# A hybrid decoder step on one core: adaLN products with the weights streaming, feature chunks further apart, and some steps of the mix phase moved

## The reference

```
shift, scale, gate = split(silu(c) @ w_ada + b_ada, 3)          # c: 9 conditions (1 prompt, 8 samples), w_ada 1024 x 3072
h = rmsnorm(x, norm_gain) * (1 + scale) + shift
qa, ka, va, za, qb, fb, ib, zb, ga, gb = split(h @ w_in)         # 9216 columns
branch A: three head groups of dilated window attention (dilation 1, 4, 16), QK-normed, ALiBi;
          the groups' results are joined with weights from their softmax denominators; * silu(za); @ w_branch_a
branch B: gated recurrence (HGRN2), chunkwise; rmsnorm; * silu(zb); @ w_branch_b
y = x + gate * ((sigmoid(ga) * A + sigmoid(gb) * B) @ w_out)
```

## Time and profile before

| | us |
|---|---|
| median of 3 runs (lowest, highest) | 3126.55 (3123.8, 3127.46) |
| the profiled execution | 3124.32 |
| its span | 3122.5 |
| input phase, up to the first product of the weave | 0 to 110.2 |
| weave | 110.2 to 2121 |
| mix | 2121 to 2724 |
| tail | 2724 to 3122.5 |
| PE busy, PEld busy, DVE busy | 2919.9, 2609.9, 1361.6 |

### The profile page before, as it was taken

One profiled execution on the slowest core, in us unless ns is written; L12 is line 12 of the kernel. 1 busy time (PEld: TensorE's weight loads), 2 busy tenths in 40 slices (PEclk: granted clock), 3 DMA queues, 4 the chain that ended last, 5 costly groups with the idle time before them and its releaser, 6 DMA issues. The chain is left out here.

```text
span 3122.5 us, 47274 instructions
## 1 busy us (share of the span) xinstructions
PE 2919.9 (94%) x18020; PEld 2609.9 (84%) x18020; DVE 1361.6 (44%) x3061; ACT 1085.1 (35%) x2165; POOL 836.7 (27%) x704
## 2 busy tenths in 40 slices
PE   7889999999999899999999999995979889589999
PEld 7778998888888799999999999993656656389999
DVE  2584334566544233343565645422434334433333
ACT  1343213444444333212444444442534434221110
POOL 0242333555422222232555533210011112040000
PEclk9999999999999999999999999997989797799999
DMA  6364432332322432322333232227676776353432
GB/s 195 95 178 137 125 95 77 105 98 92 104 99 88 166 113 94 111 84 88 95 100 102 90 100 94 98 71 263 240 262 224 254 246 212 123 194 109 126 119 86
DMA packets 385264, 417.90 MB, mean 134 GB/s; under 512 B 115600, under 2 KB 296080, under 8 KB 378384
## 3 DMA queue, kind: packets, MB, share of 16 engines
q1 hardware_dynamic: 378128, 406.24, 41.0%
q10 hardware_dynamic: 6912, 8.65, 0.8%
HBM read 284.11 MB, written 130.70 MB: 133 GB/s over the span
## 5 line engine op out<-in xcount | busy, mean ns | idle before, releaser
L667 PE MATMUL weave_bank<-h_high,w_high 128*128 128x352 f32 (+2 forms) x2240 | 819.8, 366 | 15.2 <-issue 11.4
L669 PE MATMUL weave_bank<-h_high,w_low 128*128 128x352 f32 (+2 forms) x2240 | 801.4, 358 | 0.0
L668 PE MATMUL weave_bank<-h_low,w_high 128*128 128x352 f32 (+2 forms) x2240 | 799.1, 357 | 0.0
L944 POOL TENSOR_TENSOR w_low<-weave_w_raw,w_high 128x512 fp32r<-128x512 f32 x284 | 379.9, 1349 | 771.1 <-ACT w_high L815 769.2
L667 PEld LDWEIGHTS weave_bank<-h_high,w_high 128*128 128x128 f32 x2240 | 427.0, 191 | 57.5 <-issue 14.7
L669 PEld LDWEIGHTS weave_bank<-h_high,w_low 128*128 128x128 f32 x2240 | 426.0, 190 | 40.4
L668 PEld LDWEIGHTS weave_bank<-h_low,w_high 128*128 128x128 f32 x2240 | 426.0, 190 | 39.7 <-issue 2.9
L679 PE MATMUL weave_bank<-w_high,h_high 128*128 128x256 f32 x1088 | 310.0, 285 | 0.0
L681 PE MATMUL weave_bank<-w_high,h_low 128*128 128x256 f32 x1088 | 306.7, 282 | 0.0
L680 PE MATMUL weave_bank<-w_low,h_high 128*128 128x256 f32 x1088 | 305.6, 281 | 0.0
L1671 ACT ACTIVATE mix_probs<-mix_scores,mix_o_out 128x256 f32<-128x256 f32 (+1 forms) x384 | 157.0, 454 | 319.2 <-DVE mix_o_out L1754 307.1
(11 more groups left out here) (229 smaller groups left out, 4860.6 us busy)
## 6 DMA issues: line engine op xcount, KB each, us to landing
weave_w_raw<-in_w_qkv SPq DMA_DIRECT2D x144, 256.0 KB, 2.9
mix_kv<-in_kT_c SPq DMA_DIRECT2D x24, 1024.0 KB, 7.6
mix_kv<-in_v_c SPq DMA_DIRECT2D x24, 1024.0 KB, 7.1
tail_gates<-scratch_gates SPq DMA_DIRECT2D x48, 352.0 KB, 3.2
weave_w_raw<-in_w_g SPq DMA_DIRECT2D x64, 256.0 KB, 3.0
weave_w_raw<-in_w_b SPq DMA_DIRECT2D x60, 256.0 KB, 2.8
scratch_sums<-mix_o_out SPq DMA_DIRECT2D x48, 264.0 KB, 6.0
mix_rows<-scratch_sums SPq DMA_DIRECT2D x24, 528.0 KB, 6.8
```

What stands on the lines that cost most here:

```text
L667: pe.matmul(dst, w_high[:, i, k, :], h_high[:, k, tok], start=(k == 0), stop=False)
L668: pe.matmul(dst, w_high[:, i, k, :], h_low[:, k, tok], start=False, stop=False)
L669: mm = pe.matmul(dst, w_low[:, i, k, :], h_high[:, k, tok], start=False, stop=(k == KD - 1))
L944: pool.tensor_tensor(w_part(w_low, p), w_raw[p % RAW][:, :, :], w_part(w_high, p), ALU.subtract).then_inc(w_low_done, 1)
```

## The change

It has three parts.

*Input.* The roles in the conditions' products are exchanged: the 9 conditions are the stationary operand, and 256 columns of `w_ada` stream. 12 tiles of 1024 KB take the place of 24 of 512 KB, in 4 buffers instead of 5. A product's result is [9, 256]; ACT copies it to SBUF (`copy_row`), and PE turns it in two transposes of [9, 128] back into the layout that the rest expects. The turns of tile n stand behind the product of tile n + 1, so those of tile 7, the last of shift and scale, stand behind the first gate tile. On SP, `ones`, `eps` and the identity are loaded behind the first tile and the first chunk, not behind five tiles and at the end.

*Weave.* SP loads the constants first. Chunk f now begins at unit `2 + 3 f // 2` instead of `f`, so that two chunks are spread over three units; the table `F_AT` gives the chunk of a unit.

*Mix.* The sample parts begin at step 8 instead of 4. In the first half of the joins of pairs 0 to 2, all that follows the load of the rows stands 5 steps later.

```diff
-    TILES, MOD, WBUF, POOL_KD, PIECES = 24, 16, 5, 4, 4
+    TILES, MOD, WBUF, POOL_KD, PIECES, WIDE = 12, 8, 4, 4, 4, 2 * P
...
                 def load_w(n):
                     if n >= WBUF:
-                        sp.wait_ge(ada_done, n - WBUF + 1)
-                    lo = P * (n % 4)
-                    sp.dma_start(w_ada[n % WBUF][:, :, :], dr["w_ada"][n // 4][:, :, lo:lo + P]).then_inc(w_in[n % WBUF], 16)
+                        sp.wait_ge(row_done, n - WBUF + 1)
+                    lo = WIDE * (n % 2)
+                    sp.dma_start(w_ada[n % WBUF][:, :, :], dr["w_ada"][n // 2][:, :, lo:lo + WIDE]).then_inc(w_in[n % WBUF], 16)
...
-                def vector(n):
+                def row(n):
                     pe.wait_ge(w_in[n % WBUF], 16 * (n // WBUF + 1))
-                    dst = ada_ps[:, n, :] if n < MOD else gate_ps[:, n - MOD, :]
+                    if n >= 2:
+                        pe.wait_ge(row_copied, n - 1)
                     for k in range(KD):
-                        mm = pe.matmul(dst, w_ada[n % WBUF][:, k, :], c_act[:, k, :], start=(k == 0), stop=(k == KD - 1))
+                        mm = pe.matmul(row_ps[n % 2][:, :], c_act[:, k, :], w_ada[n % WBUF][:, k, :], start=(k == 0), stop=(k == KD - 1))
+                    mm.then_inc(row_done, 1)
+
+                def vectors(n):
+                    pe.wait_ge(row_copied, n + 1)
+                    for b in range(2):
+                        dst = ada_ps[:, 2 * n + b, :] if n < MOD else gate_ps[:, 2 * (n - MOD) + b, :]
+                        mm = pe.transpose(dst, row_sb[n % 2][:, b * P:(b + 1) * P], t["ident"][0:9, 0:9])
                     mm.then_inc(ada_done, 1)
...
-                for n in range(TILES):
-                    vector(n)
-                    if n in (3, 7, 11):
-                        sums(n // 4)
+                pe.wait_ge(ident_in, 16)
+                for n in range(TILES + 1):
+                    if n < TILES:
+                        row(n)
+                    if n:
+                        vectors(n - 1)
+                    if n in (1, 4, 6):
+                        sums((1, 4, 6).index(n))
...
+                def copy_row(n):
+                    act.wait_ge(row_done, n + 1)
+                    if n >= 2:
+                        act.wait_ge(ada_done, n - 1)
+                    act.copy(row_sb[n % 2][:, :], row_ps[n % 2][:, :]).then_inc(row_copied, 1)
...
+        F_AT = {2 + 3 * f // 2: f for f in range(FT)}
...
-                    if 1 <= U < FT + 1:
-                        feature_sums(U - 1)
+                    if U - 1 in F_AT:
+                        feature_sums(F_AT[U - 1])
...
-    at = lambda i, k: 4 + SPAN * i + k * SPAN // PARTS
+    at = lambda i, k: 8 + SPAN * i + k * SPAN // PARTS
...
-    turn_at = lambda jp, half: start(jp, half) + (12 if jp < PAIRS - 1 else 6 + 2 * half)
+
+    later = lambda jp, half: 5 if jp < PAIRS - 1 and half == 0 else 0
+    turn_at = lambda jp, half: start(jp, half) + later(jp, half) + (12 if jp < PAIRS - 1 else 6 + 2 * half)
     J_LOAD = {start(*x): x for x in J_HALVES}
-    J_LEAST = {start(*x) + 2: x for x in J_HALVES}
+    J_LEAST = {start(*x) + later(*x) + 2: x for x in J_HALVES}
...
```

More of the change, by code:

```diff
@@ L68, in phase_input @@
         w_raw = [sb(f"w_raw{i}", [P, 4, P], F32) for i in range(PIECES)]
-        w_ada = [sb(f"w_ada{i}", [P, KD, P], F32) for i in range(WBUF)]
+        w_ada = [sb(f"w_ada{i}", [P, KD, WIDE], F32) for i in range(WBUF)]
+        row_sb = [sb(f"row{i}", [9, WIDE], F32) for i in range(2)]
         x_sb = [sb(f"x_sb{i}", [P, KD, CHUNK[i][1]], F32) for i in range(TCH)]
@@ L74, in phase_input @@
         ada_ps, gate_ps = ps("ada_ps", [P, 16, 9], F32), ps("gate_ps", [P, 8, 9], F32)
+        row_ps = [ps(f"row_ps{i}", [9, WIDE], F32) for i in range(2)]
         ss_ps = [ps(f"ss_ps{i}", [P, CH], F32) for i in range(2)]
@@ L179, in high @@
                     act.copy(h_high[:, :, cols(c)], x_sb[c][:, :, :]).then_inc(high_done, 1)
+                def copy_row(n):
[3 more added lines that the diff above has]
+                    act.copy(row_sb[n % 2][:, :], row_ps[n % 2][:, :]).then_inc(row_copied, 1)
                 square(0)
+                copy_row(0)
+                copy_row(1)
+                root(0)
                 square(1)
-                root(0)
+                for n in (2, 3, 4):
+                    copy_row(n)
+                root(1)
                 square(2)
-                root(1)
+                copy_row(5)
+                copy_row(6)
                 root(2)
+                copy_row(7)
                 for p in range(PIECES):
@@ L623, in recurrence @@
                         sp.dma_start(dr["branch"][4 + h][:, j * CH:j * CH + n], o_sb[:, 0:n]).then_inc(o_stored, 16)
-                for p in range(4, 7):
-                    load(p)
-                for f in range(FX):
-                    load_x(f)
                 for dst, src in CONSTANTS:
                     sp.dma_start(dst, dr[src]).then_inc(const_in, 16)
+                load_x(0)
+                load(4)
+                load_x(1)
+                load(5)
+                load(6)
+                for f in range(2, FX):
+                    load_x(f)
                 for U in range(len(STEPS)):
@@ L633, in _ @@
                         leave(U - 2)
-                    if FX <= U + 1 < FT:
-                        load_x(U + 1)
-                    if 5 <= U < FT + 5:
-                        store_x(U - 5)
+                    if U + 1 in F_AT and F_AT[U + 1] >= FX:
+                        load_x(F_AT[U + 1])
+                    if U - 5 in F_AT:
+                        store_x(F_AT[U - 5])
                     for p in pieces_at(U):
@@ L916, in _ @@
                 for U in range(len(STEPS)):
[L917 to L922 removed]
+                    if U - 4 in F_AT:
+                        feature_high(F_AT[U - 4])
+                    if U in F_AT:
+                        feature_square(F_AT[U])
+                    if U - 2 in F_AT:
+                        feature_root(F_AT[U - 2])
                     if is_a("normed", U):
@@ L1332, in phase_mix @@
     J_HALVES = [(jp, half) for jp in range(PAIRS) for half in range(2)]
-    turn_at = lambda jp, half: start(jp, half) + (12 if jp < PAIRS - 1 else 6 + 2 * half)
+    later = lambda jp, half: 5 if jp < PAIRS - 1 and half == 0 else 0
+    turn_at = lambda jp, half: start(jp, half) + later(jp, half) + (12 if jp < PAIRS - 1 else 6 + 2 * half)
     J_LOAD = {start(*x): x for x in J_HALVES}
-    J_LEAST = {start(*x) + 2: x for x in J_HALVES}
-    J_EXP = {start(*x) + 3: x for x in J_HALVES}
-    J_WEIGHT = {start(*x) + 4: x for x in J_HALVES}
-    J_SUM = {start(*x) + (7 if x == (PAIRS - 1, 1) else 5): x for x in J_HALVES}
+    J_LEAST = {start(*x) + later(*x) + 2: x for x in J_HALVES}
+    J_EXP = {start(*x) + later(*x) + 3: x for x in J_HALVES}
+    J_WEIGHT = {start(*x) + later(*x) + 4: x for x in J_HALVES}
+    J_SUM = {start(*x) + later(*x) + (7 if x == (PAIRS - 1, 1) else 5): x for x in J_HALVES}
     S_LAST = [at(i, PARTS - 1) for i in range(SB // 2)]
```

40 lines of the change are left out of this document (17 added, 23 removed).

## The result

The changed kernel took 3050.47 us (median of 4 runs, 3038.48 to 3052.42), against 3125.18 for the kernel before on the same chip: a ratio of 0.9754, 95% interval 0.9731 to 0.9777. The profiled execution took 3052.42 with a span of 3050.6. The forecast was 3031, with 3010 to 3068 as its range: the direction and the places are right, a fifth of the gain is missing, and the time lies nearer to rival 1 (3060) than to the forecast.

A forecast was written before the change was run, and what follows sets the result against it. PE, busy for 94% of the span, was taken as the bound, so its waits and needless work could give: input 30, weave 20, mix 44, sum 94 us, forecast 3031 us, range 3010 to 3068.

The forecast's parts named there:

- rival 1: Mix: keys miss their parts by 10 us, clock falls each time, gain 15 instead of 44; 3060 us, chance 0.14.
- Input phase, -30: Input phase: row products at the upper clock let the weave begin at 80.6 instead of 110.2 us, saving 30 us.
- Rival 2: Input phase: clock stays at its lower level with 9 stationary columns, phase gains 2 us; 3063 us, chance 0.18.
- Weave, -20: Weave's beginning: 8.0 us from constants first, 8 from spread chunks, 4 from the clock; bounds 8 and 24.
- the 4 us taken for the clock: Weave: clock fell with each wait (0.93 against 0.97); 5% of 125 us is 6, of which 4 was taken.
- the prediction's own mark: Weave: sign expected if right, PE's waits at the squares' sum under 5 us in total.
- Mix, -44: Mix: three later joins give 39 us, the samples' start 6, new load order costs 1; bounds 15 and 56.
- the clock's term: Mix joins: less time at the lower clock, 2 us at the first, 7 and 5 at the second and third.
- the prediction's own marks: Mix joins: PE's key wait over 10 us, or joins holding DVE for 10, would prove the step arithmetic wrong.
- The samples' start: Mix's start: four plain steps now come before the part that needs the first keys, saving 6 us.
- Rival 3: Mix: PE waits 16 us at six sample stages loaded behind a job's load; slower, 3132 us, chance 0.03.
- rival 4: Weave and mix: no new wait at the keys, all chunk waits gone; 3012 us, chance 0.04.

## Why the prediction was right, and where it failed

**What bounds the kernel:** right. Nearly all of the gain came from PE's still time and from work PE no longer does; the weave's 4.4 us of busy time are within what executions differ by.

**Input phase, -30:** right, 31.5. PE began at 12.44 (12), a tile's products took 3.62 us (3.7), the tiles stand 3.77 apart, and their records start 0.22 apart, so a pair of turns costs 0.3 and not 0.5. The modulation began at 52.98 instead of 56, the chain behind it took 25.0 instead of 23.9 (to 73.61 + 4.40 = 78.01), and POOL's low part ends last. Rival 2 is out: with nine stationary columns and 256 streaming the clock rose within the first tile (6.2 us, 9.86 less 3.62, where the lower clock throughout was put at 6.8). How much of the 31.5 us the exchanged roles gave and how much the earlier start no run tells; by the rows the modulation begins 29.1 us earlier, and PE's first product 8.0. The oscillation of which the Trainium skill tells ("TensorE: Matmul & The Clock Gate", section "HAM oscillation — how this bites in real kernels") did not come: the tiles followed each other without a wait.

**Weave, -20:** within its bounds, half right in its reasons, and in part luck. The constants' wait of 8.0 us is gone, and DVE begins 7 us after the barrier. Of the 4 us taken for the clock the 4.4 less of busy time is no proof, as seven profiles of this weave differ by 11.7 in it. And of the other 11.9 us I took 8 as saved by a lower load of DVE; 10.2 are left, against under 5 in the prediction's own mark. The load alone was the wrong view: it counts DVE's busy share and not that the fold takes 1.54 us instead of 0.41 beside POOL.

**Mix, -44:** the size failed, 26.7. The step that failed is the clock's term: "of that only part is lost ... between nothing and 12 us each, I take 7 and 5", and 2 at the first join. I took the lower clock to go with the long wait. It fell in the long waits that were left and at the short ones that came in, 1.28 us for DVE, 3.27 at the turns, and PE's busy time stayed. The two rows of steps 64 to 72 show the size that this can have: 12 us behind a wait that the prediction did not count at all. The smaller errors: the new key waits were 5.95, none and 10.57 instead of 6, 4 and 6. At the third I took the rows as the last that is waited for; a pair of keys stands behind them on SP (issued at 2506.84), and PE's next part needs it. By the prediction's own marks, a wait of over 10 there and one of DVE of over 7 (7.57), its step arithmetic is wrong at this place. And the turns' waits grew by 5.4, because the moved first half now meets the second half's join. The samples' start gave 6.6 us where 6 was taken (up to step 49, by the starts of the steps).

**Rivals.** Rival 1 (waits under another name, the clock falling each time) was part of what happened, and 0.14 was too little for it. Rival 3 did not come: no stage behind a job's load kept PE for 16 us. Nor did rival 4: new waits for the keys came, and 10.2 us of the chunk waits stayed.

## What to carry to other kernels

A wait's price on PE is its length and the stretch at the lower clock that may follow it, and in these profiles the second did not shrink with the first (17.0 to 30.7 us, and once none, behind a wait of 1.27 or 1.28): when a change turns one long wait into two short ones, leave the clock's part out of the gain until PE's busy time for the same records shows it. When a consumer is moved back in a queue of transfers, ask for each transfer now behind it who waits for that, and move the partner (here the second half's join) as well. An engine's busy share says nothing of a wait that comes from its operation being slowed; compare one operation's shortest and longest duration first.

## What was not expected of the hardware

- PE stood still for 1.28 us, and the clock was down for 17.0 us behind it in one kernel and 30.7 in another; with products in that gap it stayed up in three profiles. But it also stayed up once behind 1.27 us with nothing in the gap. What decides between the two is open.
- It also fell at step 160 with no wait of over 0.7 us in the 15 us ahead, in two kernels (27.3 us each). What brought it down there is open.
- One fold on DVE takes 0.41 us alone and 1.54 beside POOL. The Trainium skill ("Trainium Architecture — The Big Picture", section "What this means for kernel authors") says that within the engines' side of SBUF only VectorE and GpSimd contend, by a lock on the ports they share; these rows agree: the fold of 119.31 ends at 120.85, just behind POOL's operation (120.57).
- The weave with the same instructions took 1981.1 to 1992.2 us in seven profiles; PE's busy time in it varied with it (1943.6 to 1955.3), its still time less (47.8 to 50.9). A change of under 10 us in this stage needs its waits and its still time read, not its length.
